# Attention value sums scaled on ScalarE and gated four heads at a time on VectorE, in a hybrid decoder step

## The reference, cut to what matters

```python
def attend_with_sinks(q, kk, vv, mask, sinks):
    s = jnp.einsum('...qgrd,...kgd->...grqk', q, kk) * (A_HEAD_DIM ** -0.5)
    s = jnp.where(mask, s, -jnp.inf)
    m = jnp.maximum(jnp.max(s, axis=-1, keepdims=True), sk)
    p = jnp.exp(s - m)
    denom = jnp.sum(p, axis=-1, keepdims=True) + jnp.exp(sk - m)
    p = (p / denom).astype(vv.dtype)
    return jnp.einsum('...grqk,...kgd->...qgrd', p, vv)

def merge(x, attn, ret, ga, gb, w_out):
    ret = rms_norm(ret).reshape(N, T, B_V_WIDTH).astype(x.dtype)
    mixed = jnp.concatenate([jax.nn.silu(ga) * attn, jax.nn.silu(gb) * ret], axis=-1)
    return x + jnp.einsum('nte,ed->ntd', mixed, w_out)
```

## Time and profile before

| | us |
|---|---|
| median of three timed executions | 1908.94 |
| lowest, highest | 1907.4, 1910.17 |
| the profiled execution, whole | 1902.62 |
| its span, first to last instruction | 1900.8 |
| TensorE matmul busy | 1750.4 (92%) |
| VectorE busy | 1386.5 (73%) |
| ScalarE busy | 825.5 (43%) |
| mean granted TensorE clock | 0.983 |

### The profile page before, as it was taken

The page is one execution under the profiler, slowest core; times in us unless marked ns, Lnnn a source line. Parts: engine busy times, 40 slices in busy tenths (PEclk is TensorE's granted clock), DMA queues, the critical chain, the costliest instruction groups (busy, mean ns, idle before and its releaser), DMA issues.

```text
span 1900.8 us, 35728 instructions
## 1 busy us (share of the span) xinstructions
PE 1750.4 (92%) x11512; PEld 947.5 (50%) x11512; DVE 1386.5 (73%) x4768; ACT 825.5 (43%) x1917; POOL 68.5 (4%) x108
## 2 busy tenths in 40 slices
PE   0778899999999999988998989999899999999999
PEld 0345555554555455543445555555455555555444
DVE  4768999987665766678875899998866676667442
ACT  2556566653443334332443556665344333442010
POOL 3010000000000000011001000000100000000000
PEclk9798999999999999999999999999999999999999
DMA  5874455466114211179893454554611143115774
GB/s 152 207 186 72 88 106 110 99 135 154 31 33 125 72 44 33 32 207 275 254 263 129 80 106 92 111 112 87 187 31 33 42 111 87 32 33 134 207 214 144
DMA packets 419520, 220.92 MB, mean 116 GB/s; under 512 B 360257, under 2 KB 391169, under 8 KB 419265
## 3 DMA queue, kind: packets, MB, share of 16 engines
q1 hardware_dynamic: 346336, 168.41, 36.7%
q0 software_dynamic: 9728, 35.66, 5.7%
q10 hardware_dynamic: 63360, 15.74, 5.0%
HBM read 88.75 MB, written 49.68 MB: 73 GB/s over the span
## 4 chain that ended last, share of the span: by engine, by line
PE 45%; DVE 31%; DMA 7%; ACT 6%; issue 5%; SPq 3%; ACTq 1%; DVEq 0%; POOL 0%
PE PB L550 19%; PE PA L550 19%; DMA r<-r 5%; DVE w_mx L907 3%; DVE r L1096 2%; DVE r L1053 2%; PE OB L724 1%; PE S L704 1%; DVE r L1200 1%; DVE mix L1171 1%; PE S L742 1%; PE OB L732 1%; DVE land L1039 1%; DVE r L1058 1%; DVE w_a L924 1%
## 5 line engine op out<-in xcount | busy, mean ns | idle before, releaser
L550 PE MATMUL PB<-w_a,hT 128*128 128x512 f16 (+1 forms) x1920 | 403.9, 363 | 0.0
L550 PE MATMUL PA<-w_a,hT 128*128 128x512 f16 (+1 forms) x1920 | 401.9, 360 | 0.0
L550 PEld LDWEIGHTS PB<-w_a,hT 128*128 (+1 forms) x1920 | 186.5, 99 | 182.4 <-issue 15.4
L550 PEld LDWEIGHTS PA<-w_a,hT 128*128 (+1 forms) x1920 | 185.9, 99 | 176.3 <-issue 5.4
L550 PE MATMUL PA<-w_b,r 128*128 128x512 f16 x768 | 172.7, 382 | 14.5 <-DMA r<-r 11.6
L1862 ACT ACTIVATE w_a<-land 128x1024 uint16<-128x1024 uint16 x60 | 63.4, 1057 | 279.4 <-DVE land L1211 267.8
L550 PE MATMUL PB<-w_b,hT 128*128 128x512 f16 x768 | 175.9, 379 | 0.3 <-DVE r L1200 0.3
L550 PE MATMUL PA<-w_b,hT 128*128 128x512 f16 x768 | 173.3, 381 | 0.0
L550 PE MATMUL PB<-w_b,r 128*128 128x512 f16 x768 | 171.3, 379 | 1.1 <-DVE r L1335 1.1
L1779 ACT ACTIVATE r<-r,nm,unqk 128x256 f32<-128x256 f32 x192 | 112.6, 588 | 45.5 <-DVE sd L1109 45.5
L550 PEld LDWEIGHTS PA<-w_b,r 128*128 128x128 f16 x768 | 74.5, 98 | 108.5 <-DMA r<-r 13.4
(11 more groups left out here) (268 smaller groups left out, 2858.0 us busy)
## 6 DMA issues: line engine op xcount, KB each, us to landing
out<-r SPq DMA_DIRECT2D x40, 512.0 KB, 4.7
r<-mixed SPq DMA_DIRECT2D x32, 512.0 KB, 4.2
w_b<-in_w_in POOLq DMA_DIRECT2D x16, 512.0 KB, 8.8
mixed<-mix SPq DMA_DIRECT2D x32, 256.0 KB, 2.0
mixed<-mix SPq DMA_DIRECT2D x64, 128.0 KB, 1.8
w_a<-in_w_in POOLq DMA_DIRECT2D x16, 512.0 KB, 7.8
w_b<-in_w_out POOLq DMA_DIRECT2D x16, 512.0 KB, 7.8
r<-in_x_prompt SPq DMA_DIRECT2D x16, 512.0 KB, 4.5
```

Of the source, the lines that this page charges most:

```text
L550: last = nc.tensor.matmul(out[0:s.rows, 0:n], lhs, w16(ph, k, p, wpart), start=(k == 0 and part == 0 and wpart == 0), stop=(k == KT - 1 an ...
```

## The change

It has three parts.

1. ScalarE gets `a_scale`: for one group of a tile it waits for the value sums (a_pv) and the third link of the reciprocal chain (ch_amx), and for group 0 for the store of the buffer (mix_out); then four copies bring the heads' 64 columns out of the bank into `mix`, scaled by the reciprocal row sum. In a step, group 0 stands between `a_phi` and the second weight piece, group 1 between exp of group 1 and `a_tanh`. For tile 15 both stand before B0's `b_vg` of T0, for the last tile after `b_planes` of T1.
2. VectorE's `a_mix` of a prompt tile becomes one product of `mix` with the gate per group (128 x 256, in place), which waits for `a_scale`. The twelve links and the rotation run first, with nothing woven in but the weight piece; then both products, then the gate.
3. In B0 and B1, `b_decay` of T1 comes before the sample's gate, and the eight maxima are spread: 0 and 1 where four stood; 2, 3 in step 4 and 5, 6 in step 5, between `b_decay` and the gate; 4 and 7 after these steps.

The sample tile's own mixing is as before.

```diff
+        def mixed_heads(x, s, c0, g):
+            return x[:, s.par, c0 + 2 * g * A_DIM:c0 + A_W].rearrange("p (a n) -> p a n", n=2 * A_DIM)[:, 0:3:2, :]
...
                 else:
-                    for h in range(A_GROUP):
-                        last = a_mix_head(s, g, h)
-                    last.then_inc(a_mx, 1)
+                    v.wait_ge(a_sc, 2 * tn(L, s) + g + 1)
+                    m = mixed_heads(mix, s, 0, g)
+                    V.tensor_tensor(m, m, mixed_heads(land, s, A_W + 2 * KV_W, g), ALU.mult).then_inc(a_mx, 1)
...
                     if not u.sample:
-                        a_mix_open(L, u, 0, m0)
-                        a_mix_head(u, 0, 0)
-                        a_norm_link(s, ch, 0)
-                        a_mix_head(u, 0, 1)
...
-                        a_norm_link(s, ch, 11)
+                        for i in range(RSQRT_LINKS + 1):
+                            a_norm_link(s, ch, i)
+                            if i == 3 and k is not None:
+                                w_low(L, "B0", k, 0)
                         a_rotate(L, s, ch)
+                        a_mix(L, u, 0, m0)
+                        a_mix(L, u, 1, m1)
                         gate("A", L, s, 2, A_W, A_W + 2 * KV_W)
...
                     b_decay(ph, L, s - 1)
+                    for q in rows:
+                        w_absmax(L, nxt, q)
                     gate(ph, L, s, 1, 256, 768)
...
                     b_rope(ph, L, S)
+                    b_decay(ph, L, T1)
                     gate(ph, L, S, 1, 256, 768)
-                    b_decay(ph, L, T1)
...
-                    for q in range(4):
+                    for q in range(2):
                         w_absmax(L, nxt, q)
...
                     for c in range(4, CV0):
-                        b_step(ph, mid(c))
+                        b_step(ph, mid(c), rows=((2, 3), (5, 6))[c - 4] if c < 6 else ())
                         if c < 6:
-                            w_absmax(L, nxt, 2 * c - 4)
-                            w_absmax(L, nxt, 2 * c - 3)
+                            w_absmax(L, nxt, 3 * c - 8)
...
+            def a_scale(L, s, g):
+                n = 2 * an(L, s) + g
+                act.wait_ge(a_pv, n + 1)
+                act.wait_ge(ch_amx, 3 * n + 3)
+                if g == 0:
+                    act.wait_ge(mix_out[s.par], 16 * mix_count("A", L, s))
+                for h in range(A_GROUP):
+                    m = (h // 2 * A_GROUP + 2 * g + h % 2) * A_DIM
+                    last = A.activation(mix[:, s.par, m:m + A_DIM], OO[g][:, h * A_DIM:(h + 1) * A_DIM], ACT.Copy,
+                                        scale=rr[:, g, h:h + 1])
+                last.then_inc(a_sc, 1)
...
                     a_exp(L, t, 0)
                     a_phi(L, t, 0)
+                    if not u.sample:
+                        a_scale(L, u, 0)
                     if k is not None:
                         w_high(L, "B0", k, 1)
                     a_exp(L, t, 1)
+                    if not u.sample:
+                        a_scale(L, u, 1)
                     a_tanh(L, s)
...
                 F = mid(STEPS - 1)
+                a_scale(L, E - 1, 0)
+                a_scale(L, E - 1, 1)
                 b_vg("B0", L, T0)
                 b_tout("B0", L, T0)
                 for g in range(2):
                     act.wait_ge(a_tp[g], 16 * (L + 1) * TILES)
                 b_planes("B0", L, T1)
+                a_scale(L, E, 0)
+                a_scale(L, E, 1)
                 b_vg("B0", L, T1)
```

More of the change, by code:

```diff
@@ L341, in trunk @@
         alone_count = sem("alone_count")
+        a_sc = sem("a_values_scaled")
         ch_wm, ch_ws = sem("chain_w_max"), sem("chain_w_scale")
@@ L1136, in a_mix @@
                         a_rr_link(s, g, ch, i)
-                ch.wait()
-                v.wait_ge(a_pv, n + 1)
-                if g == 0:
+                if s.sample:
+                    ch.wait()
+                    v.wait_ge(a_pv, n + 1)
+                if s.sample and g == 0:
                     v.wait_ge(mix_out[b], 16 * mix_count("A", L, s))
@@ L1575, in layer, with b_step @@
                 b_mix("B0", L, T0)
-                def b_step(ph, s, k=None):
+                def b_step(ph, s, k=None, rows=()):
                     nxt = "B1" if ph == "B0" else "O"
```

## The result

The changed kernel takes 1943.3 us in the median against 1908.17 us before: a ratio of 1.0182, 95% interval 1.0163 to 1.0202, 35 us slower. The forecast was slower by 24 us, 1933 us with a range of 1908 to 1950. So sign and range hold, and the size is 11 us short. One of the changed kernel's four executions took 6868.61 us: the ratio leaves it out, the median counts it (without it the median is 1942.33 us), and nothing here explains it.

What follows compares the result with a forecast made beforehand. The prediction took a loop through VectorE and ScalarE, not TensorE's work, to bound attention. Layer 0 15.5, layer 1 12, retention entries 8, less 12 in retention, made about +24 us: 1933 us, range 1908 to 1950.

Steps and rivals of the forecast that it cites:

- The loop through ScalarE in layer 0: Layer 0 attention: exp 0 to gate grows from 8.19 to 9.63 us, +1.44 per conversion step; 15.5 us for the stage.
- The price of the copy: ScalarE in attention: 128x64 copies from PSUM at 0.20 us spacing, so a group of four ends after 0.9 us.
- VectorE's saving: VectorE in attention steps: eight operations become two, norm and mixing go from 4.05 to 3.75 us, only 0.3 us back.
- The round trip: Attention, ahead of tanh: ScalarE stands still while VectorE makes its product and hands back, 0.5 us.
- Layer 1: Layer 1 attention: exp 0 to gate 8.70 now, 9.63 after, +0.93 in eight steps; 12 us for the stage.
- The entry: Into retention, once a layer: holds from scaling tile 15 and the last tile overlap; 4 us later, twice, 8 us.
- Retention: Four retention blocks: two maxima later shorten TensorE's waits for the sample's state update, 3.0 us a block, 12 us gained.
- Operation count: Attention rival: fewer VectorE operations decide, the handover hides, and the kernel gets faster, 1893 us; chance 0.14.
- Cancelling: Attention rival: copy groups of 0.5 us take 20 us off, so the time is 1912 or 1909 us; chance 0.08.
- That the maxima move no wait: Retention rival: the second wait only takes the first's place, 12 us less gained, 1945 us; chance 0.05.
- The clock: Attention rival: new TensorE waits of 2 to 3 us lower its clock, costing perhaps 9 us more, 1942 us; chance 0.13.
- Three marks of a right forecast: Attention profile signs: copies at about 0.2 us spacing, tanh idle 0.5 us for VectorE's product, VectorE idle before the gate.

Runs made afterwards that it cites:

- dose: Kernel before, with four extra 128x64 copies from SBUF to SBUF on ScalarE ahead of tanh in steps 4 to 15 of both layers: 1927.92 us.
- Experiment 4: Changed kernel, with group 1's scaling ahead of its exponentials and both VectorE products ahead of the rotation: 1926.48 us.
- experiment 9: Changed kernel, with tile 15 alone mixed by VectorE's head operations at the entry into retention: 1939.16 us.
- experiment 10: Changed kernel, with the last tile alone mixed by VectorE's head operations at the entry into retention: 1933.93 us.
- experiment 3: Changed kernel, with tile 15 and the last tile both mixed by VectorE's head operations, ScalarE scaling nothing for them: 1928.58 us.
- experiment 5: Changed kernel, with ScalarE scaling group 0 only; VectorE's head operations mix group 1, and tile 15 and the last tile wholly: 1896.94 us.
- experiment 7: Kernel before, with only the eight maxima of each retention block spread: 1892.79 us.
- experiment 1: Kernel before, with parts 1 and 2 of the change alone, retention as before: 1952.95 us.
- the decay alone: Kernel before, with only the decay of T1 moved ahead of the sample's gate: 1908.53 us.

## Why the prediction was right in sign and short in size

- **The loop through ScalarE in layer 0: right.** The forecast was +1.44 a step; the interval from exp 0 to the gate grew by 1.36 to 1.45, and exp 0 follows exp 0 19.02 us on (five steps from 269.23 to 364.31) instead of 17.54 (261.39 to 349.08), +1.48. The stage lost 16.2 us (15.5). Its split holds in the main, read from exp 0 to exp 0: steps 4 to 7 lost 4.2 us (forecast 3.2), steps 8 to 12 7.4 (7.2), steps 13 to 15 3.5 (5.1), and step 16, which the forecast left out, 1.4. The last three were taken at 16.45 us a step before the change; from exp 0 to exp 0 they took 16.56, 17.39 and 16.56, and 18.0 each after.
- **The price of the copy: right.** 0.20 us of spacing, 0.89 to 0.93 us a group, where 0.20 and 0.9 were taken. The Trainium skill's figures (ScalarE: Activation LUTs, § What ACT_TABLE_LOAD costs), from which 1.05 us a group were estimated, are not met by the copies out of PSUM; the dose's, whose source is SBUF, took 1.05.
- **VectorE's saving: right, and worth nothing.** Links and products now take 3.7 us (310.13 to 313.13, and two spacings of 0.34) where links and heads took 4.05 and 3.75 were forecast. The Trainium skill's rule to minimize the number of operations (VectorE: DVE Perf Modes, § Rules for kernel authors) finds no support here: six fewer gave 0.4 us, and none of it reached the gate.
- **The round trip: right.** 0.5 us forecast, 0.49 and 0.55 measured as idle ahead of tanh, 27 times, 14.4 us in all. Experiment 4, which removes it by order alone, gives back 17 us.
- **Layer 1: the step that failed in size.** "8.70 now, 9.63 after: +0.93 per step" took exp 0 to the gate as the same sum of ScalarE operations as in layer 0. It measured 9.94, since the weight piece on VectorE starts 3.84 us behind exp 0 in layer 1 and 3.10 in layer 0 (1262.82 and 310.84), so ScalarE's group ended with 0.32 us left to wait. A further 0.38 us came in behind plane 0, where the transposed plane lands later; why was not tried. Six steps from exp 0 at 1202.14 to 1316.50 give 19.06 us each against 17.49, +1.57. From exp 0 to exp 0, steps 8 to 15 lost 11.5 us (forecast 7.4), the earlier ones 6.8 (4.5), and step 16, not forecast, 2.7, of which 2.2 fall behind the last transposes and so count with the entry.
- **The entry: the step that failed most.** "The two overlap; an end 4 us later, twice: 8 us." They do not overlap (experiments 9 and 10), and of tile 15's hold the prediction named the wrong victim. It priced TensorE's bank behind `b_vg`, and missed that `a_plo` of the last tile, and so the last transposing DMA, is queued behind `a_mix` of tile 15 on VectorE. Measured: 7.4 and 8.3 us, 7.7 us more than the 8 forecast. Of this the two holds made 12.6 us, counted from exp 0 of the last tile; the other 3.1 are the slower last attention step, which stood in neither term of the sum.
- **Retention: right.** 12 us forecast, 6.5 + 6.2 in the trace, and 13.6 us in the run of part 3 alone. Half of what the trace gained is regained clock, more than the 0.7 of 3.0 us a block that the forecast gave it, and half is shorter waits. In layer 0 it is not steady from one trace to another: experiments 3, 5 and 7, with the same spreading, gained 2.5 to 3.1 us there. The decay's order is worth nothing, as stated.
- **The rivals.** Operation count (0.14) is refuted: handover and copies are not hidden. Cancelling (0.08) fell with the copies' 0.91 us. That the maxima move no wait (0.05) fell with experiments 1 and 7. The clock (0.13) changed a little: the attention stages were granted 0.95 and 0.98 instead of 0.97 and 1.00. It came out as a consequence and not as the price: the interval from exp 0 to the gate, which holds only ScalarE's and VectorE's work, grew by 1.36 to 1.45 us of the 1.48 that a step of layer 0 grew.
- Three marks of a right forecast were met: 0.20 spacing, tanh waiting for VectorE's product, VectorE waiting ahead of the gate. The bookkeeping of the miss: entries +7.7 (holds 4.6, last attention steps 3.1), layer 1 +6.8, start and output stage +2, layer 0 +0.7, retention -1; together some 16 us on the profiled executions, of which the low profiled execution of before is 5.

## What to carry to other kernels

Moving work to a less busy engine pays only if that engine has a wait at the very place where the work goes in: the same group of copies was free behind the high plane and cost its full time ahead of tanh. A step of work that crosses to another engine and back before the next instruction may start costs the handover each time; look for what was long done and can be asked for earlier, as experiment 4 did with a mere change of order. At the seam between two stages read the whole program of each engine behind every new wait, not only the consumer you have in mind: two holds there were worth 2.5 to 3.8 us each, and they added.

## What the runs showed of the hardware

TensorE's clock fell to the lower of its two levels (1.2 of 2.4 GHz) for part of a 3 us stretch after it had waited 2.12 us for the scores; twelve matmuls took 2.74 us, which otherwise take 1.48:

```profile
302.72 0.28 PE L645 MATMUL S<-kT_hi,r 64*128 64x256 f16 x2 [2.12 <-DVE r L1032]
...
304.45 2.74 PE L555 MATMUL PA<-w_a,hT 128*128 128x256 f16 x12
```

```profile
303.00:306.00 3.00, 3.00 (x32) 1.99 (x27) 3.00 (x9) 0.00 (x0) 0.00 (x0) 0.63 1.13 209
```

The wait alone does not explain it: one step earlier the same wait of 2.12 us (before 283.51) left the clock at 1.00. The step from transposes to transposes was then 20.3 us and the next one 18.2, its wait 1.16 instead of 2.12 us. The scores followed 19.30 us on (322.02) where they had followed after 19.21, so the lower clock cost next to nothing there: the next wait took up most of the 1.3 us.

Four copies of 128x64 took 0.91 us from PSUM to SBUF and 1.05 us from SBUF to SBUF.

VectorE's four head operations run without links between them took 0.86 us, hardly less than ScalarE's 0.91, and the product of four heads 0.42.

The output stage with the start of layer 1's attention varies from one execution to another by several us: from the last values of layer 0's retention to the first transposes of layer 1 it took 225 us in the trace of before and 230 in that of the decay alone, whose code there is the same, and 237 with the dose. With the dose, TensorE was idle 3.2 us more in this stretch and busy 8.6 us more with the same work, at a granted clock of 0.94 instead of 0.98 (columns as in the earlier trace rows; before, then the dose):

```profile
815.82:1040.77 224.95, 203.56 (x1089) 96.46 (x1089) 174.31 (x461) 82.49 (x120) 22.57 (x33) 0.98 0.83 236
```

```profile
824.62:1061.36 236.74, 212.19 (x1090) 99.42 (x1088) 174.32 (x461) 82.48 (x120) 22.56 (x33) 0.94 0.82 224
```

So most of the 12 us is clock. With the decay alone it is about half and half: 2.3 us more busy at 0.96, 2.7 more idle, and the waits for DMAs (line 550) are 15.9 us instead of 11.6. What lowers the clock there no run shows. A lag must be read by place; the difference of two spans would have mispriced the dose by 12 us.
